# Two conditioning projections of a two-block kernel: cut into tiles and put beside later stages

## The reference

```
mod   = silu(c)     @ ada_w + ada_b      # ada_w is 1024 x 6144
cmod  = silu(c_ctx) @ ada_w + ada_b      # context tokens
shift1, scale1, gate1, shift2, scale2, gate2 = split(mod, 6)
h     = rms_norm(x) * (1 + scale1) + shift1       # context: columns of cmod
y     = mixer(h)              # gated delta rule + retention, each gated by h @ w
x     = x + gate1 * (y @ w_out)
x     = x + gate2 * swiglu(rms_norm(x) * (1 + scale2) + shift2)
```

## Time and profile before

| | us |
|---|---|
| runs, median (lowest to highest of 3) | 5458.54 (5451.34 to 5460.92) |
| the profiled execution | 5466.76 |
| its span | 5465.0 |
| busy: PE, DVE, ACT, Pool | 4778.6, 2305.1, 1375.0, 581.4 |
| PE, weights against (silu(c), silu(c_ctx)), 768 passes | 183.4 |
| idle of PE before them | 38.3 |

### The profile page before, as it was taken

One profiled execution on the slowest core, in us unless ns is written; L12 is line 12 of the kernel. 1 busy time (PEld: TensorE's weight loads), 2 busy tenths in 40 slices (PEclk: granted clock), 3 DMA queues, 4 the chain that ended last, 5 costly groups with the idle time before them and its releaser, 6 DMA issues. The chain is left out here.

```text
span 5465.0 us, 48366 instructions
## 1 busy us (share of the span) xinstructions
PE 4778.6 (87%) x19724; PEld 3309.6 (61%) x19724; DVE 2305.1 (42%) x4163; ACT 1375.0 (25%) x2632; POOL 581.4 (11%) x494
## 2 busy tenths in 40 slices
PE   7897778997899999797979897779777799899998
PEld 3454566474688888556564345554464655688886
DVE  1476664214422222439393105560476722433334
ACT  1342112112221111322221103340263621322222
POOL 0001332111000000004040000001000000000000
PEclk9799899999899999799989998889898999999999
DMA  6213222111111111110000011001100002111111
GB/s 211 85 47 106 75 66 85 41 31 77 39 54 47 47 51 39 51 31 1 23 1 23 24 34 32 12 1 35 35 1 12 1 24 81 29 49 47 47 51 58
DMA packets 256366, 246.41 MB, mean 45 GB/s; under 512 B 15600, under 2 KB 246000, under 8 KB 254736
## 3 DMA queue, kind: packets, MB, share of 16 engines
q1 hardware_dynamic: 255088, 216.97, 13.0%
q0 software_dynamic: 1056, 26.35, 1.2%
HBM read 224.42 MB, written 18.87 MB: 45 GB/s over the span
## 5 line engine op out<-in xcount | busy, mean ns | idle before, releaser
L193 PE MATMUL bank<-h,wslot 128*128 128x512 f32 (+1 forms) x2048 | 842.1, 571 | 26.8 <-DVE Y L211 18.0
L193 PEld LDWEIGHTS bank<-h,wslot 128*128 128x128 f32 x2048 | 392.4, 192 | 459.0 <-issue 447.4
L193 PE MATMUL bank<-hT,wslot 128*128 128x512 f32 (+1 forms) x1088 | 442.1, 564 | 31.3 <-DMA hT<-hspill 20.6
L193 PEld LDWEIGHTS bank<-hT,wslot 128*128 128x128 f32 x1088 | 209.7, 194 | 255.4 <-issue 228.0
L211 DVE SCALAR_TENSOR_TENSOR x<-bank,mod,x 128x512 f32<-128x512 f32 x224 | 168.0, 750 | 387.7 <-PE bank L193 387.5
L193 PE MATMUL bank<-ffn2h,wgh 128*128 128x512 f32 x704 | 277.2, 394 | 16.5 <-DVE ffn2l L211 16.0
L193 PE MATMUL bank<-ffn1h,wfh 128*128 128x512 f32 x704 | 277.4, 394 | 16.2 <-DVE ffn1l L211 15.6
L193 PE MATMUL bank<-ffn1l,wfh 128*128 128x512 f32 x704 | 275.8, 392 | 0.0
L193 PE MATMUL bank<-ffn1h,wfl 128*128 128x512 f32 x704 | 275.7, 392 | 0.0
L193 PE MATMUL bank<-ffn2l,wgh 128*128 128x512 f32 x704 | 275.6, 391 | 0.0
L193 PE MATMUL bank<-ffn2h,wgl 128*128 128x512 f32 x704 | 275.5, 391 | 0.0
(11 more groups left out here) (491 smaller groups left out, 9088.7 us busy)
## 6 DMA issues: line engine op xcount, KB each, us to landing
wslot<-in_w_in SPq DMA_DIRECT2D x40, 1024.0 KB, 5.4
wslot<-in_ada_w SPq DMA_DIRECT2D x24, 1024.0 KB, 5.2
wslot<-in_w_mod SPq DMA_DIRECT2D x24, 1024.0 KB, 5.2
wslot<-in_w_ffn_in SPq DMA_DIRECT2D x44, 512.0 KB, 5.0
wslot<-in_ffn_w_gate SPq DMA_DIRECT2D x22, 512.0 KB, 4.0
wslot<-in_ffn_w_up SPq DMA_DIRECT2D x22, 512.0 KB, 5.3
hT<-hspill POOLq DMA_DIRECT2D x2, 5120.0 KB, 15.6
wslot<-in_w_ffn_out SPq DMA_DIRECT2D x20, 512.0 KB, 3.4
```

Of the source, the lines that this page charges most:

```text
L193: return Counted() if counting[0] else self.q.matmul(o, l, r, start=start, stop=stop)
```

## The change

- Block 1's projection does only groups 0 to 7 (shift1 and scale1) in stage a, four before the norm sums and four behind. x comes in three transfers on ACT's queue, and the squares wait for each. "ab" waits for ranges of columns of h instead of for the whole stage.
- Block 2's projection leaves stage gs: no `cond()`. The chain gets five banks, begin three. `begin(s+2)` moves in front of `uu(s+1)` on PE, `kkeq(s+2)` in front of "plus u" on DVE.
- `AdaTiles` does the rest, a tile of 128 columns at a time: Pool loads 512 KB into one of two buffers (rows of 512 bytes) and multiplies by silu(c) of each row; DVE sums the 8 parts into 128 x 128; PE sums over partitions with a column of ones; DVE adds the bias.
- Block 1's other 32 tiles go into gate1 (0 to 6), behind each rotary tile (7 to 26) and beside the first products after them (27 to 31). Block 2's 64 tiles go into ffn1, three per f.

```diff
+    class AdaTiles:
+        def fetch(self, e, t):
+            s = self.aw.take(t)
+            for ev in self.aw.freed(t):
+                e.wait_ge(*ev)
+            m = self.todo[t][0]
+            e.dma_start(s[:, :].rearrange("p (k m) -> p k m", m=128),
+                        self.ada.w[:, m * 128:(m + 1) * 128].rearrange("(k p) m -> p k m", p=128)).then_inc(self.aw_in[t % 2](t), 16)
+        def pool(self, e, n):
+            for t in n:
+                if t == n[0] == 0:
+                    self.fetch(e, 0)
+                if t + 1 < len(self.todo):
+                    self.fetch(e, t + 1)
...
+                e.wait_ge(*self.aw_in[t % 2].after(t))
+                e.tensor_tensor(v, v, self.ada.scv[:, :, self.todo[t][1]].unsqueeze(2).to_broadcast([128, 8, 128]), OP.mult).then_inc(self.st.pool("p", t), 1)
+        def dve(self, e, n):
+            for t in n:
...
+                e.wait_ge(*self.st.pool.after("p", t))
+                e.reduce_sum(a[:, :], self.aw[t][:, :].rearrange("p (k m) -> p m k", m=128)).then_inc(self.st.dve("r", t), 1)
+                self.aw.give((t,), self.st.dve.now())
+                if t >= self.lag:
+                    self.bias(e, t - self.lag)
...
+        def pe(self, e, n):
+            for t in n:
...
+                e.wait_ge(*self.st.dve.after("r", t))
+                e.matmul(b[:, 0:1], self.acc[t][:, :], ones[:, 0:1]).then_inc(self.st.pe("c", t), 1)
 def a_pe
-        for g in range(12):
+        for g in range(4):
             ad1.pe(e, g)
         rms1.pe(e)
-        for g in range(12, 25):
+        for g in range(4, 9):
 def a_act
+        for i, (n0, n) in enumerate(ALL):
+            e.dma_start(xa[...][:, :, n0:n0 + n], io["xcatT"][:, :, n0:n0 + n]).then_inc(xa_in[i]("in"), 16)
 def gp_pe
-        barrier(e, n1, ad1.st)
+            e.wait_ge(*nm1.ready(0 if c < 2 else 256 if c < 6 else 768))
 gs: banks, PE's step, DVE's step
-    bk_m, bk_b, bk_c2 = Ring(bank[0:4]), Ring(bank[4:6]), Ring(bank[6:8])
+    bk_m, bk_b = Ring(bank[0:5]), Ring(bank[5:8])
                 v2(s + 1)
-                cond()
-                uu(s + 1)
             if s < 8:
                 begin(s + 2)
             if s < 9:
-                cond()
+                uu(s + 1)
                 new(s + 1)
...
+            if s < 8:
+                kkeq(s + 2)
             if s < 9:
-                cond()
                 for d in range(2):
                     plus("u", s + 1, d, Va)
-            if s < 8:
-                kkeq(s + 2)
 Gate.pe, Gate.dve
+                    if self.tiles and (m, n0) != (0, 0):
+                        self.tiles.pe(e, [m * 2 + n0 // 512 - 1])
...
+                    if self.tiles and (m, n0) != (3, 512):
+                        self.tiles.dve(e, [m * 2 + n0 // 512])
 rp_pe, rp_dve, rp_pool
                 rotate(RT[j - 1])
+                at1.pe(e, [6 + j])
...
+                if hf == 0 and c < 6:
+                    at1.pe(e, [26 + c])
...
+            at1.dve(e, [7 + RT.index(t)])
+        at1.dve(e, range(27, 32))
...
+            at1.pool(e, [7 + RT.index(t)])
+        at1.pool(e, range(27, 32))
 Ffn.pe, Ffn.dve, Ffn.pool
+                if self.ada and kind == "u" and m and f:
+                    self.ada.pe(e, range(3 * f - 3, 3 * f))
...
+                if self.ada and kind == "u":
+                    self.ada.dve(e, range(3 * f, min(3 * f + 3, len(self.ada.todo))))
...
+                if self.ada:
+                    self.ada.pool(e, range(3 * f, min(3 * f + 3, len(self.ada.todo))))
 ffn1
+    at2 = ffn1.ada = AdaTiles("at2", ad2, [(m, 1) for m in range(16)] + [(m, 0) for m in range(48)], ffn1.bk, 3)
+        ad2.act(e)
```

More of the change, by code:

```diff
@@ L341, in __init__ @@
             self.mv = mod[:, :].rearrange("p (m w) -> p m w", w=2)
-            self.rows = [row[0:2, 0:256], row[0:2, 256:512]]
+            self.rows = [row[0:2, 0:256], row[0:2, 256:512]] if ng else []
         def sp(self, e, g):
@@ L388, in done, with __init__, bias @@
         def done(self):
-            return self.st.dve.after("mod", 23)
+            return self.st.dve.after("mod", self.ng - 1)
+    class AdaTiles:
+        def __init__(self, nm, ada, todo, bk, lag):
+            self.nm, self.ada, self.todo, self.bk, self.lag, self.st = nm, ada, todo, bk, lag, Stage(nm)
+            self.aw, self.acc = Ring([sb(f"{nm}w{i}", [1024]) for i in range(2)]), Ring([sb(f"{nm}a{i}", [128]) for i in range(lag + 1)])
+            self.aw_in = [Sem(f"{nm}in{i}", 16) for i in range(2)]
+        def fetch(self, e, t):
[11 more added lines that the diff above has]
+                    self.fetch(e, t + 1)
+                v = self.aw[t][:, :].rearrange("p (k m) -> p k m", m=128)
+                e.wait_ge(*self.aw_in[t % 2].after(t))
+                e.tensor_tensor(v, v, self.ada.scv[:, :, self.todo[t][1]].unsqueeze(2).to_broadcast([128, 8, 128]), OP.mult).then_inc(self.st.pool("p", t), 1)
+        def dve(self, e, n):
+            for t in n:
+                a = self.acc.take(t)
+                for ev in self.acc.freed(t):
+                    e.wait_ge(*ev)
+                e.wait_ge(*self.st.pool.after("p", t))
[3 more added lines that the diff above has]
+                    self.bias(e, t - self.lag)
+                if t == len(self.todo) - 1 and self.lag == 1:
+                    self.bias(e, t)
+        def bias(self, e, t):
+            m, w = self.todo[t]
+            at = self.ada.pb + m
+            e.wait_ge(*self.st.pe.after("c", t))
+            e.tensor_tensor(self.ada.mv[:, m, w:w + 1], self.bk["ada", t][:, 0:1], par[:, at:at + 1], OP.add).then_inc(self.st.dve("mod", t), 1)
+            self.bk.give(("ada", t), self.st.dve.now())
+        def pe(self, e, n):
+            for t in n:
+                b = self.bk.take("ada", t)
+                for ev in self.bk.freed("ada", t):
+                    e.wait_ge(*ev)
+                e.wait_ge(*self.st.dve.after("r", t))
+                e.matmul(b[:, 0:1], self.acc[t][:, :], ones[:, 0:1]).then_inc(self.st.pe("c", t), 1)
+                self.acc.give((t,), self.st.pe.now())
@@ L397, in __init__, with act @@
             self.st, self.nm, self.x, self.nk, self.rngs, self.inv, self.rstd, self.banks = st, nm, x, nk, rngs, inv, rstd, banks
-        def act(self, e):
-            for n0, n in self.rngs:
+        def act(self, e, there=()):
+            for i, (n0, n) in enumerate(self.rngs):
+                if there:
+                    e.wait_ge(*there[i])
                 for k in range(self.nk):
@@ L511, in build @@
     bk_a = Ring(bank)
-    ad1 = Ada("ad1", io["ada_w"], "ada_b", "c", "c_ctx", mod1, sc1, row, bk_a)
+    ad1 = Ada("ad1", io["ada_w"], "ada_b", "c", "c_ctx", mod1, sc1, row, bk_a, 8)
     n1 = Stage("n1")
-    xa_in, hs_out = Sem("xa", 16), Sem("hspill", 16)
+    xa_in, hs_out = [Sem(f"xa{i}", 16) for i in range(3)], Sem("hspill", 16)
     xav, (h1, h1c) = views(xa)[0], views(hT)
@@ L522, in a_sp @@
         e.dma_start(par[:, :], io["par"]).then_inc(par_in("in"), 16)
-        e.dma_start(xa[:, :].rearrange("p (k t) -> p k t", t=TT), io["xcatT"]).then_inc(xa_in("in"), 16)
-        for g in range(24):
+        for g in range(8):
             ad1.sp(e, g)
@@ L547, in a_dve @@
         consts(e)
-        for g in range(12):
+        for g in range(4):
             ad1.dve(e, g)
         rms1.dve(e)
-        for g in range(12, 25):
+        for g in range(4, 9):
             ad1.dve(e, g)
         e.wait_ge(*ad1.done())
+        for x in xa_in:
+            e.wait_ge(*x.after("in"))
         nm1.dve(e)
@@ L902, in chunk @@
                 e.dma_start(vb[d][:, :], io["vspill"][c * 128:(c + 1) * 128, :]).then_inc(vb_in[d](s), 16)
-        chunk(0)
-        for g in range(10):
-            ad2.sp(e, g)
         for s in range(10):
[L908 to L912, removed]
+            chunk(s)
     def gs_pe(e):
         barrier(e, gp)
[L916 to L921, removed]
         def begin(s):
@@ L1103, in gs_dve @@
         e.wait_ge(*vs_out.after(11))
[L1104 to L1109, removed]
         def grid(t):
@@ L1226, in gs_dve @@
                                 nbet[quarter(q), c * 8 + 4:c * 8 + 8].unsqueeze(2).to_broadcast([32, 4, 32]), OP.mult).then_inc(gs.dve("wb", c, q), 1)
-        for i, _ in enumerate(sub(0)):
-            if i >= 5 and i % 4 == 1:
-                cond()
+        for _ in sub(0):
+            pass
         kkeq(0)
@@ L1353, in __init__ @@
             self.rsts = Ring([sb(f"r{nm}{i}", [NL]) for i in range(2)])
-            self.bk = Ring(bank)
+            self.bk, self.tiles = Ring(bank), None
         def at(self, x, n0, n):
@@ L1447, in build @@
     (hb, hbc) = views(hT2)
+    bk_r = Ring(bank)
+    at1 = AdaTiles("at1", ad1, [(m, 0) for m in range(16, 48)], bk_r, 1)
     mg = mark()
     gg1 = Gate("gate1", 1536, hb, yg, "gdn_norm_g", lambda x, n0: [], [lambda: h2_in.after("in")])
+    gg1.bk, gg1.tiles = bk_r, at1
     drop(mg)
@@ L2191, in dve @@
```

(6 more changed lines are left out.)

46 lines of the change are left out of this document (21 added, 25 removed).

## The result

| | us |
|---|---|
| runs before, median (lowest to highest of 4) | 5459.73 (5451.34 to 5467.72) |
| runs after, median (lowest to highest of 4) | 5663.92 (5658.94 to 5666.61) |
| ratio | 1.0373, 95% interval 1.0355 to 1.0391 |
| profiled execution after, its span | 5658.94, 5657.1 |

The forecast was 5612 in a range of 5500 to 5760. The kernel became 204 us slower; some 150 was forecast.

A forecast was written before the change was run, and what follows sets the result against it. PE was taken as the bound, without a gap in feed-forward. From the profiled 5466.8 us, -81 -11 -9 -38 -32 +2 +88 +230 +1 = +150 gives 5617, or 5608 against the median; forecast 5612, range 5500 to 5760.

The forecast's parts named there:

- Removed at the start: Stage a: with eight of 24 projection groups left, the modulation starts about 75 to 83 us, not 158.5; taken -81 us.
- overlap for ab: Small product after the modulation: waiting for column ranges instead of the whole stage, it ends at 38.4, not 49.0; -11 us.
- the shared case: Start of the kernel: first weight load shares bandwidth with x on ACT's queue and lands at about 14 us, otherwise still 22.4.
- The delta rule: Delta-rule stage without 24 groups: -9 before the chain, -38 in steps without DVE's pieces, -32 with them; taken -79 us.
- The rival that the reorder does nothing: Delta rule: the reorder does not shorten the steps; gains 40 us less, time 5652; 8 in 100.
- Gate 1: Gate 1 stage, tiles 0 to 6: only the small matmuls show; +2 us (0 to 10).
- Rotary stage: Tiles 7 to 31: PE waits each time for rotate, sin, sum and reduction in series; +88 us (60 to 130).
- the clock: Rotary stage: PE's idle of 3.3 in 11 us may lower its granted clock; 10 us taken, 0 to 30.
- Feed-forward: Feed-forward 1, 64 tiles: DVE waits for Pool, delaying the weight cut; stalls 168, matmuls 17, clock 45; +230 us (140 to 470).
- The covered chain: Rival, feed-forward: the three tiles end before PE wants the next weights, time 5404; 14 in 100 including its neighbours.
- The issue by rows: Rival, Pool's loads: each 1024-row issue takes 5.6 us, not 1.0; time 5925, or 5770 at half; 12 in 100.
- the clock is never withdrawn: Rival, rotary stage and feed-forward: PE's idle does not lower its clock; 55 us less, time 5557; 18 in 100.

## Why the prediction was right, and where its sizes were off

The sign, the mechanisms and the places were right; the time came out 52 above the point and inside the range. By the table of starts the excess stands in two stretches, 28 in the rotary stage and 23 in feed-forward.

- *Removed at the start.* -78.8 to the modulation where -81 was taken, and 10.4 of overlap for ab where 11 was. The first weights landed at 15.4, near the 14 of the shared case.
- *The delta rule.* The step of 24.9 was 24.7, with luck inside it: the order and the third bank were taken as 2.7 (9.0 less 6.3) and gave 2.2, and the groups gave 8.4 where 7.6 was left for them. The stage gained 79.5 where 79 was taken. By the copies of "new" the steps without DVE's pieces gave 38.9 of it (38 taken), three of the four with pieces 25.3 (8 each taken), and what lies before the first copy, with the fourth of them, 15.4 (9 and 8 taken). That the three with pieces gave 9.9, 6.4 and 9.0 is not explained by these runs. The rival that the reorder does nothing is refuted; with the banks it was worth 25 of this.
- *Gate 1.* +5.4 against +2: two waits of 1 us, seven small matmuls of about 0.2 each, and some 2 us in a slower first product and two loads that PE waits for in before too. Of the stretched DVE instructions that the prediction allows for, the trace has one, 1.8 longer, at 780.55. DVE then works without a gap up to the reduction that PE waits 1.06 for, so by the timeline that wait comes from it.
- *Rotary stage.* The chain was named correctly: 3.4 to 3.8 of idle, 20 times, against 3.3. The 110 between this stage and its version with PE asking later are 73.6 of waiting, with 3.2 of that in the last tiles where 6 was taken, and 36.3 of clock; the small matmuls are 5.7. The term that was mis-sized is the clock, taken as 10 and given 0 to 30: it lies outside that bound. The row that I had beside it said 2.3 for one cold start in feed-forward; 20 such waits would have been 46, and I did not carry it over.
- *Feed-forward.* Waits of 7.5 and 12.3 in place of 6.6 and 10.7, 189 in 22 waits in place of 168. The term behind that is DVE's reduction: taken as 1.3, bound 2.0, measured 1.92, three in each chain. Pool's product (2.1 taken, 1.92 measured) and its issue (1.0 and 0.92) were near, and the landing 4.6 for 5.0. The matmuls were 15.6 against 17. The clock cost 47.8, against 45.
- *The rivals.* The covered chain did not occur, and the kernel with Pool ahead shows that it needed no less work, only a third buffer and another order. The issue by rows is refuted at 0.92 for 1024 rows. That the clock is never withdrawn is refuted: 0.88 and 0.91.
- *Who excludes whom.* I wrote that the exclusion of DVE and Pool adds nothing in feed-forward because DVE waits there. That held for this kernel alone: as soon as Pool works ahead it costs the cut 1.4 us, without a wait of PE behind it in the trace.

## What to carry to other kernels

An engine that is idle three quarters of a stage is no cover if it works in order and the filler makes it wait for another engine: put the filler where its input is already there, one piece behind each piece of the main work, and ask for its result one step later. Price a handover chain by its round trip (issue, product, reduction, back), not by the busiest engine in it; here 4.8 us of work per tile in turn cost 250 us and the same work unrolled cost 16. Idle on PE is paid twice, once as waiting and once as clock: here 48 us on top of 191 in feed-forward, and 36 on top of 74 in the rotary stage, where the waits were shorter and closer together.

## What the hardware showed that was not expected

- A DVE reduction of 128x1024 to 128x128 in float32 takes 1.92 us with a stride of 512 bytes and 1.22 without. A Pool product of the same size takes 1.92 with plain and 2.11 with strided output.
- The issue of a transfer of 1024 rows on Pool takes 0.92 us; 128 rows took 0.54 and 0.71.
- Useless matmuls in PE's waits made a kernel 45 us faster: the granted clock was 1.00 in two stretches where it had been 0.88 and 0.91. Without them the same matmuls had taken 36 and 48 us longer in these two stages.
- A DVE instruction with two SBUF inputs took 2.12 in place of 0.68 beside a Pool product.
